# Two transformer blocks with a top-2-of-8 expert layer on one core: the first expert piece in banks 4 to 7, no scatter in the first turn, scatter halves and last transposes at other weight slots

## The chip, the core and the metric

One core of a Trainium2 chip runs the whole program. Its engines are PE (TensorE, the matrix engine), DVE (VectorE), ACT (ScalarE), POOL (GpSimd) and SP (SyncE, which here only issues DMAs). Matmul results go to PSUM, which has 8 banks of 128 x 512 float32. The metric is the device time of one execution in microseconds, lower is better.

## What is computed

Two blocks over 256 tokens of width 1024. The first has two layers of a hybrid mixer, a dense feed-forward after the first and a mixture of experts after the second. The second block has two dense feed-forwards around a mixer. The change touches the mixture of experts alone:

```python
def moe_swiglu(x, w_router, w1, w3, w2):
    logits = einsum('nd,de->ne', xf, w_router)
    top_logits, top_idx = lax.top_k(logits, 2)     # 2 of 8 experts for each token
    gates = softmax(top_logits)
    ...
    h = silu(xb @ w1[e]) * (xb @ w3[e])            # 1024 -> 3584
    y = h @ w2[e]                                  # 3584 -> 1024
    out = out.at[tok].add(y * gate)
```

## The kernel before

**Expert turns.** Each expert takes one pass over up to 128 gathered tokens, called a turn (`it` in the code, 0 to 7 here; the last has `is_last`). The weights of an expert come as 42 weight slots of 1 MB, each as two DMAs of 512 KB issued by SP into a ring of 6 buffers (`ring_data`). A slot's buffer is loaded again when PE has used it (`ring.used`). The hidden width of 3584 is cut into four pieces `c` (widths 1024, 1024, 1024, 512). An `up` slot `(c, m)` multiplies the gathered tokens by 128 rows (256 for piece 3) of w1 and w3; a `down` slot adds two 128-row parts of w2 to the expert's output. The order of a turn is written out in `Wide.TURN`: up 1 (8 slots), down 0 (4), up 2 (8), down 1 (4), up 3 (4), down 2 (4), `next` 0 (8 slots: up piece 0 of the next expert), down 3 (2). In the text "up 1,3" is slot `("up", 1, 3)`. Since a turn computes piece 0 of the next expert, piece 0 of the first expert (8 slots) stands before turn 0.

**Arithmetic of a slot.** Weights and activations are split into a high and a low part. ACT makes the high part (`weights_hi`, `e_high`, L2129), DVE the low part (`weights_lo`, `e_low`, L2456), both three slots ahead of PE (`Wide.LEAD`). PE then issues 12 matmuls of 128 x 512: 8 with the high weights (L1490 and L1491 for up, L1517 and L1518 for down), 4 with the low weights (L1494 and L1522). The 4 low ones of a slot stand in the timeline as one row "x4", so the distance from one x4 row to the next is the time of a slot.

**Banks.** An up slot accumulates in banks 0 to 3, a down slot in banks 4 and 5. Banks 6 and 7 serve all else: the gather, the transposes of a finished piece (`turn_h`, L1478), and the scatter (`scatter`, L1468 and L1469), which adds the previous expert's gated output (`Y_hi`, `Y_lo`) to the tokens by a matmul with the 0/1 matrix `chosen`. After an up piece, ACT takes the Silu of banks 0 and 1, DVE multiplies by banks 2 and 3 (`multiply`, L2915, semaphore `moe_h`), PE transposes the product, ACT and DVE copy it as high and low part (`turned`, `turned_low`, L2921, semaphore `moe_hT`).

**Where the scatter stands.** PE scatters token half 0 before slot up 1,4 and half 1 before up 1,6; both write banks 6 and 7, so the second waits until DVE has added the first to `yacc` (`add`, L2909, semaphore `y_added`). In turn 0 there is no previous expert: DVE sets `chosen`, `Y_hi` and `Y_lo` to zero before the first slots (L2977 to L2979), and turn 0 scatters zeros.

**Engines' programs.** Each engine runs its own program in order: PE, ACT and DVE each loop over turns 0 to 6 with `Fori(0, last)` and have the last turn written out behind it. `last` is read from memory into a register of each engine (`value_load`).

## Time and profile before

| | |
|---|---|
| median of 3 runs | 2168.39 us (2162.72 to 2168.89) |
| the profiled execution | 2169.8 us, of which the span from first to last instruction is 2168.0 us |
| mean granted TensorE clock | 0.990 of full |
| expert turns | from about 584 to 1562 us of the span |
| DMA in the expert turns | about 370 GB/s |

The times come from three executions; the trace is of one more. A row of the timeline is: start in us, duration in us, engine, line, operation, output<-inputs, count, and in square brackets the idle time of the engine just before, with what released it. The time shown for a matmul is longer than the distance to the next one (0.39 us against 0.227), since matmuls overlap; the distances between starts count.

### The profile page before, as it was taken

The page shows a single profiled execution, that of the slowest core. Times are in us where ns is not written, and L with a number is a line of the kernel's source. Part 1 is how long each engine was busy: PE and PEld are TensorE (multiplying, and loading weights), DVE is VectorE, ACT ScalarE, POOL GpSimd, SP SyncE. Part 2 cuts the span into 40 slices and gives each one's busy share as a digit, 9 for nine tenths or more (in the row PEclk, how much of TensorE's full clock was granted, in tenths as well). Part 3 has the DMA queues.
Part 4 walks back from the last instruction along what each step waited for, and adds up shares of the span by engine and source line. Part 5 has one row for each costly group of instructions (what it writes and reads, how often), then busy time and mean ns, then how long its engine had stood idle before and what let it go on. Part 6 is the DMA issues. An engine that isn't in the chain of part 4 may idle for free.

```text
span 2168.0 us, 31519 instructions
## 1 busy us (share of the span) xinstructions
PE 2124.3 (98%) x11901; PEld 1775.6 (82%) x11901; DVE 1594.7 (74%) x1660; ACT 1217.6 (56%) x1210; POOL 171.0 (8%) x240
## 2 busy tenths in 40 slices
PE   9999999999899999999999999999999999989998
PEld 8987888898778888888888888788778887877887
DVE  3777454567788989989898988989865439866454
ACT  4154343415467777777777777677664423664443
POOL 1200000310200000000000000000067010000000
PEclk9999999999899999999999999999999999999999
DMA  9134555412599999999999999999946564434552
GB/s 363 61 98 165 194 188 176 142 63 96 161 334 372 356 371 374 359 379 358 374 363 372 360 376 371 349 377 364 339 140 195 194 176 159 161 107 159 191 192 80
DMA packets 244403, 542.22 MB, mean 250 GB/s; under 512 B 20214, under 2 KB 122656, under 8 KB 243936
## 3 DMA queue, kind: packets, MB, share of 16 engines
q1 hardware_dynamic: 238896, 521.37, 67.3%
q0 software_dynamic: 4448, 13.79, 2.4%
q10 hardware_dynamic: 976, 5.91, 0.7%
q8 instruction: 57, 0.93, 0.2%
q14 instruction: 26, 0.21, 0.0%
HBM read 538.64 MB, written 2.36 MB: 250 GB/s over the span
## 4 chain that ended last, share of the span: by engine, by line
PE 83%; DVE 10%; issue 3%; ACT 2%; DMA 2%; SPq 0%; DVEq 0%; ACTq 0%
PE bank L1339 9%; PE bank L1341 9%; PE bank L1340 9%; PE bank L1494 8%; PE bank L1490 8%; PE bank L1491 8%; PE bank L1065 6%; PE bank L1517 4%; PE bank L1518 4%; PE bank L1522 4%; DVE weights_lo L2456 2%; PE bank L1063 2%; PE bank L1652 2%; DMA ring_data<-in_moe_w 1%; PE bank L1132 1%
## 5 line engine op out<-in xcount | busy, mean ns | idle before, releaser
L2456 DVE TENSOR_TENSOR weights_lo<-ring_data,weights_hi 128x2048 fp32r<-128x2048 f32 x336 | 760.6, 2289 | 86.4 <-ACT weights_hi L2129 85.2
L2129 ACT ACTIVATE weights_hi<-ring_data 128x2048 fp32r<-128x2048 f32 x336 | 639.8, 1920 | 183.6 <-DMA ring_data<-in_moe_w 182.5
L1490 PE MATMUL bank<-weights_hi,xg_hi 128*128 128x512 f32 x896 | 352.5, 393 | 2.6 <-DVE arena L2915 2.6
L1491 PE MATMUL bank<-weights_hi,xg_lo 128*128 128x512 f32 x896 | 349.9, 390 | 0.0
L2451 DVE TENSOR_TENSOR weights_lo<-ring_data,weights_hi 128x2048 fp32r<-128x2048 f32 x98 | 226.5, 2342 | 49.5 <-ACT weights_hi L1904 49.5
L1494 PE MATMUL bank<-weights_lo,xg_hi 128*128 128x512 f32 x896 | 240.1, 390 | 0.6 <-DVE weights_lo L2456 0.6
L1340 PE MATMUL bank<-weights_lo,xT_hi 128*128 128x512 f32 x584 | 229.5, 393 | 0.0
L1339 PE MATMUL bank<-weights_hi,xT_hi 128*128 128x512 f32 x520 | 206.2, 397 | 1.7 <-DVE bank L2504 0.9
L1341 PE MATMUL bank<-weights_hi,xT_lo 128*128 128x512 f32 x520 | 203.1, 391 | 0.0
L1490 PEld LDWEIGHTS bank<-weights_hi,xg_hi 128*128 128x128 f32 x896 | 168.7, 188 | 37.1 <-issue 3.0
L1494 PEld LDWEIGHTS bank<-weights_lo,xg_hi 128*128 128x128 f32 x896 | 168.4, 188 | 36.3 <-DVE weights_lo L2456 1.0
L1491 PEld LDWEIGHTS bank<-weights_hi,xg_lo 128*128 128x128 f32 x896 | 168.7, 188 | 34.2
L1904 ACT ACTIVATE weights_hi<-ring_data 128x2048 fp32r<-128x2048 f32 x98 | 184.0, 1918 | 0.0
L1517 PE MATMUL bank<-weights_hi,hT_hi 128*128 128x512 f32 x444 | 174.3, 393 | 0.7 <-DVE hT_lo L2921 0.7
L1518 PE MATMUL bank<-weights_hi,hT_lo 128*128 128x512 f32 x444 | 172.9, 389 | 0.0
L1871 ACT ACTIVATE arena<-bank 128x384 f32<-128x384 f32 (+5 forms) x130 | 62.8, 502 | 169.2 <-PE bank L1065 57.3
L2472 DVE TENSOR_TENSOR hT_lo<-bank,hT_hi 128x256 fp32r<-128x256 f32 x66 | 25.0, 420 | 160.0 <-ACT hT_hi L1915 159.9
L1915 ACT ACTIVATE hT_hi<-bank 128x256 fp32r<-128x256 f32 x66 | 21.8, 382 | 209.2 <-PE bank L1360 209.2
L1065 PE MATMUL bank<-actT,ring_data 128*128 128x256 f32 x608 | 136.8, 384 | 0.0
L1065 PEld LDWEIGHTS bank<-actT,ring_data 128*128 128x128 f32 x608 | 115.7, 192 | 17.0 <-issue 0.4
L1340 PEld LDWEIGHTS bank<-weights_lo,xT_hi 128*128 128x128 f32 x584 | 111.2, 190 | 22.2
L1522 PE MATMUL bank<-weights_lo,hT_hi 128*128 128x512 f32 x444 | 118.8, 389 | 0.0
(527 smaller groups left out, 3194.2 us busy)
## 6 DMA issues: line engine op xcount, KB each, us to landing
ring_data<-in_moe_w SPq DMA_DIRECT2D x672, 512.0 KB, 4.5
ring_data<-in_ffn_w_in SPq DMA_DIRECT2D x88, 512.0 KB, 4.6
ring_data<-in_w_in SPq DMA_DIRECT2D x71, 512.0 KB, 4.4
ring_data<-in_ffn_w SPq DMA_DIRECT2D x66, 512.0 KB, 4.0
ring_data<-in_ffn_w_out SPq DMA_DIRECT2D x44, 512.0 KB, 3.9
ring_data<-in_w_out SPq DMA_DIRECT2D x24, 512.0 KB, 4.6
ring_data<-in_w_in SPq DMA_DIRECT2D x8, 396.0 KB, 4.3
ring_data<-in_w_in SPq DMA_DIRECT2D x8, 390.0 KB, 5.5
```

The lines of the kernel that those rows point to most:

```text
L1065: i = mm(bk(b, 2, T)[:, g], wt[:, k, P * g:P * g + P], actT[:, k, :], start=k == 0, stop=k == DT - 1)
L1339: mm(o, x_hi, w_hi, start=start, stop=False, **kw)
L1340: mm(o, x_hi, w_lo, start=False, stop=False, **kw)
L1341: return mm(o, x_lo, w_hi, start=False, stop=stop, **kw)
L1490: mm(o, xg_hi[:, k, :], e_hi(at)[:, r], start=k == 0, stop=False)
L1491: mm(o, xg_lo[:, k, :], e_hi(at)[:, r], start=False, stop=False)
L1494: i = mm(bank[2 * part + q][:, :], xg_hi[:, k, :], e_lo(at)[:, r], start=False, stop=k == DT - 1)
L1517: mm(o, ehT_hi[:, 2 * m + f, :], w_hi[:, f, cd], start=first and f == 0, stop=False)
L1518: mm(o, ehT_lo[:, 2 * m + f, :], w_hi[:, f, cd], start=False, stop=False)
L2129: nc.scalar.activation(e_hi(at), ring_data[:, e_slot(at), :], ACT.Copy).then_inc(ring.hi_done, 1)
L2451: v.tensor_tensor(f.lo_slot(f.n0 + at), w, f.hi_slot(f.n0 + at), ALU.subtract).then_inc(f.ring.lo_done, 1)
L2456: v.tensor_tensor(e_lo(at), ring_data[:, e_slot(at), :], e_hi(at), ALU.subtract).then_inc(ring.lo_done, 1)
```

## The change

1. The first gather writes banks 0 and 1, and piece 0 of the first expert accumulates in banks 4 to 7 (`up_slot(..., 4)`). Its Silu and product read those banks.
2. Turn 0 is written out on PE and DVE (`turn(0, False, True)`), and the loops of both run from 1. PE reads `last` behind turn 0. ACT's loop still runs from 0.
3. In turn 0 the wait for the first product stands before up 1,1 and no longer before up 1,0; there are no scatters, no adds, and no memsets of `chosen`, `Y_hi`, `Y_lo`. The semaphores get their counts from other instructions.
4. On ACT and DVE the first Silu and product come behind the tenth weight split (m = 9) and no longer before it.
5. In turns 1 to 7 scatter half 0 stands before up 1,3 instead of up 1,4, and DVE's add of it moves likewise; half 1 stays before up 1,6.
6. In the last turn the transposes of piece 3 and what follows them move from slot down 2,3 to down 2,2; on ACT and DVE they come ahead of the last weight split.

```diff
-                def up_slot(c, m, at, split):
+                def up_slot(c, m, at, split, b0=0):
...
-                        o = bank[2 * part + q][:, :]
+                        o = bank[b0 + 2 * part + q][:, :]
...
-                        if part in (("up", 1, 0), ("up", 2, 0), ("up", 3, 0), ("next", 0, 0)):
+                        if part in (("up", 1, int(is_first)), ("up", 2, 0), ("up", 3, 0), ("next", 0, 0)):
...
-                        if part == ("up", 1, 4):
-                            pe.wait_ge(sem("ysb_ready"), it * 2 + 2)
-                            pe.wait_ge(sem("pgT_ready"), it + 1)
+                        if part == ("up", 1, 3) and not is_first:
+                            pe.wait_ge(sem("ysb_ready"), it * 2)
+                            pe.wait_ge(sem("pgT_ready"), it)
                             pe.wait_ge(sem("moe_hT"), it * 4 + 1)
                             scatter(0)
-                        if part == ("up", 1, 6):
+                        if part == ("up", 1, 6) and not is_first:
                             pe.wait_ge(sem("y_added"), it * 4 + 2)
                             scatter(1)
+                        if part == ("down", 0, 0) and is_first:
+                            pe.wait_ge(sem("moe_hT"), 1)
...
-                        if part == ("next", 0, 1) or (is_last and part == ("down", 2, 3)):
+                        if part == ("next", 0, 1) or (is_last and part == ("down", 2, 2)):
...
-                    up_slot(0, m, m, FFN_LOADS + m + 1)
+                    up_slot(0, m, m, FFN_LOADS + m + 1, 4)
+                turn(0, False, True)
                 pe.wait_ge(sem("dve_stage"), stage("npass_ready"))
                 last = pe.value_load(npass_i[0:1, 1:2], min_val=E - 1, max_val=2 * E - 1)
-                with pe.Fori(0, last) as it:
+                with pe.Fori(1, last) as it:
...
-                    if m == e_first + 1:
-                        silu(0, n_moe + e_first)
+                    if m == e_first + 2:
+                        silu(0, n_moe + e_first, 4)
...
+                        if is_last and (kind, c, m) == ("down", 2, 2):
+                            turned_low(3, it * 4 + 4)
...
-                        if part == ("up", 1, 4):
+                        if part == ("up", 1, 3) and not is_first:
                             add(it, 0)
...
-                v.memset(chosen.bitcast(F32)[:, :, :], 0.0).then_inc(sem("pgT_ready"), 1)
-                v.memset(Y_hi.bitcast(F32)[:, :], 0.0).then_inc(sem("ysb_ready"), 1)
-                v.memset(Y_lo.bitcast(F32)[:, :], 0.0).then_inc(sem("ysb_ready"), 1)
+                v.tensor_scalar(yacc[:, :, :], x[:, :, :], ALPHA, None, ALU.mult).then_inc(sem("y_added"), 4)
```

Three places show how instructions move. **PE, where the first piece ends and turn 0 begins.** Before, the register load and the loop's entry stand between the last matmul of the piece and up 1,0, which waits for `moe_h`:

```order
L1494 MATMUL bank3<-weights_lo_55,xg_hi_58 128x512
L1582 TENSOR_LOAD npass_i [waits dve_stage]
L1582 ISA x2
L1583 UNCONDITIONAL_BRANCH
L1583 ISA
L1483 ISA [waits moe_h]
L1490 MATMUL bank0<-weights_hi1_49,xg_hi_58 128x512 [waits weights_hi]
```

Now the piece ends in banks 4 to 7 and up 1,0 follows at once in bank 0:

```order
L1496 MATMUL bank4<-weights_lo_55,xg_hi_58 128x512 [waits weights_lo]
L1496 MATMUL bank5<-weights_lo_55,xg_hi_58 128x512
L1496 MATMUL bank6<-weights_lo_55,xg_hi_58 128x512
L1496 MATMUL bank7<-weights_lo_55,xg_hi_58 128x512
L1492 MATMUL bank0<-weights_hi1_49,xg_hi_58 128x512 [waits weights_hi]
L1493 MATMUL bank0<-weights_hi1_49,xg_lo_59 128x512
```

The wait stands one slot later, before the transposes that stand ahead of up 1,1:

```order
L1496 MATMUL bank3<-weights_lo_55,xg_hi_58 128x512
L1478 MATMUL bank6<-consts_sb,arena 128x128 [waits moe_h]
L1478 MATMUL bank6<-consts_sb,arena 128x128 x3
L1478 MATMUL bank7<-consts_sb,arena 128x128 x4
L1492 MATMUL bank0<-weights_hi1_49,xg_hi_58 128x512 [waits weights_hi]
```

The register load and the loop's entry have moved behind the last down slot of turn 0:

```order
L1524 MATMUL bank5<-weights_lo_55,hT_hi1_50 128x512
L1588 TENSOR_LOAD npass_i [waits dve_stage]
L1588 ISA x2
L1589 UNCONDITIONAL_BRANCH
L1589 ISA
L1485 ISA [waits moe_h]
L1492 MATMUL bank0<-weights_hi1_49,xg_hi_58 128x512 [waits weights_hi]
```

**DVE, the loop body, from the choice of the next tokens (L2891, now L2899) on.** Before, four low weight parts and then the add of scatter half 0 (banks 6 and 7 into `arena`):

```order
L2891 TENSOR_SCALAR arena<-consts_sb,small 128x128
L2455 REGISTER_ALU
L2456 TENSOR_TENSOR weights_lo_55<-ring_data,weights_hi1_49 128x2048 [waits weights_hi]
L2455 REGISTER_ALU
L2456 TENSOR_TENSOR weights_lo_55<-ring_data,weights_hi1_49 128x2048 [waits weights_hi]
L2455 REGISTER_ALU
L2456 TENSOR_TENSOR weights_lo_55<-ring_data,weights_hi1_49 128x2048 [waits weights_hi]
L2455 REGISTER_ALU
L2456 TENSOR_TENSOR weights_lo_55<-ring_data,weights_hi1_49 128x2048 [waits weights_hi]
L2909 TENSOR_TENSOR arena<-arena,bank6 128x512 [waits scatter_psum]
L2907 REGISTER_ALU
L2909 TENSOR_TENSOR arena<-arena,bank7 128x512 [waits scatter_psum]
```

Now three low weight parts stand ahead of the add, and the fourth follows it:

```order
L2899 TENSOR_SCALAR arena<-consts_sb,small 128x128
L2463 REGISTER_ALU
L2464 TENSOR_TENSOR weights_lo_55<-ring_data,weights_hi1_49 128x2048 [waits weights_hi]
L2463 REGISTER_ALU
L2464 TENSOR_TENSOR weights_lo_55<-ring_data,weights_hi1_49 128x2048 [waits weights_hi]
L2463 REGISTER_ALU
L2464 TENSOR_TENSOR weights_lo_55<-ring_data,weights_hi1_49 128x2048 [waits weights_hi]
L2917 TENSOR_TENSOR arena<-arena,bank6 128x512 [waits scatter_psum]
L2915 REGISTER_ALU
L2917 TENSOR_TENSOR arena<-arena,bank7 128x512 [waits scatter_psum]
L2463 REGISTER_ALU
L2464 TENSOR_TENSOR weights_lo_55<-ring_data,weights_hi1_49 128x2048 [waits weights_hi]
```

**DVE, end of the last turn.** Before, the low part of the transposed last piece (`hT_lo`) stands behind the last three low weight parts that follow the product (bank2):

```order
L2915 TENSOR_TENSOR arena<-arena,bank2 128x512 [waits moe_silu]
L2455 REGISTER_ALU
L2456 TENSOR_TENSOR weights_lo_55<-ring_data,weights_hi1_49 128x2048 [waits weights_hi]
L2455 REGISTER_ALU
L2456 TENSOR_TENSOR weights_lo_55<-ring_data,weights_hi1_49 128x2048 [waits weights_hi]
L2455 REGISTER_ALU
L2456 TENSOR_TENSOR weights_lo_55<-ring_data,weights_hi1_49 128x2048 [waits weights_hi]
L2921 TENSOR_TENSOR hT_lo1_51<-bank6,hT_hi1_50 128x512 [waits moe_hT_hi]
L2451 TENSOR_TENSOR weights_lo_55<-ring_data,first_hi_92 128x2048 [waits weights2_hi]
```

Now it stands behind two of them, and the last one follows it:

```order
L2923 TENSOR_TENSOR arena<-arena,bank2 128x512 [waits moe_silu]
L2463 REGISTER_ALU
L2464 TENSOR_TENSOR weights_lo_55<-ring_data,weights_hi1_49 128x2048 [waits weights_hi]
L2463 REGISTER_ALU
L2464 TENSOR_TENSOR weights_lo_55<-ring_data,weights_hi1_49 128x2048 [waits weights_hi]
L2929 TENSOR_TENSOR hT_lo1_51<-bank6,hT_hi1_50 128x512 [waits moe_hT_hi]
L2463 REGISTER_ALU
L2464 TENSOR_TENSOR weights_lo_55<-ring_data,weights_hi1_49 128x2048 [waits weights_hi]
L2459 TENSOR_TENSOR weights_lo_55<-ring_data,first_hi_92 128x2048 [waits weights2_hi]
```

## Rows read from the trace of the kernel before

**Rows 1.** The page, the chain of work that ended last, by engine:

```profile
PE 83%; DVE 10%; issue 3%; ACT 2%; DMA 2%; SPq 0%; DVEq 0%; ACTq 0%
```

**Rows 2.** Windows; last three columns: granted clock, DMA share, GB/s:

```profile
610.00:620.00 10.00, 10.00 (x43) 8.17 (x43) 9.78 (x12) 8.05 (x6) 0.00 (x0) 0.84 0.58 185
640.00:740.00 100.00, 100.00 (x464) 83.19 (x463) 88.32 (x55) 75.06 (x54) 1.07 (x1) 1.00 1.00 375
870.00:880.00 10.00, 9.86 (x44) 7.82 (x43) 8.90 (x8) 5.92 (x5) 0.00 (x0) 1.00 0.84 304
```

**Rows 3.** Timeline of PE where the loop goes from turn 0 to 1:

```profile
731.05 1.07 PE L1522 MATMUL bank<-weights_lo,hT_hi 128*128 128x512 f32 x4
733.77 1.07 PE L1494 MATMUL bank<-weights_lo,xg_hi 128*128 128x512 f32 x4
```

**Rows 4.** Timeline of DVE ahead of its first weight parts:

```profile
587.41 0.27 DVE L2977 MEMSET chosen<- 128x256 f32 x1
...
589.74 15.44 DVE L2456 TENSOR_TENSOR weights_lo<-ring_data,weights_hi 128x2048 fp32r<-128x2048 f32 x7
```

**Rows 5.** Timeline of PE, first piece and start of turn 0:

```profile
588.59 1.07 PE L1494 MATMUL bank<-weights_lo,xg_hi 128*128 128x512 f32 x4
592.02 1.19 PE L1494 MATMUL bank<-weights_lo,xg_hi 128*128 128x512 f32 x4 [0.56 <-DVE weights_lo L2456]
...
605.77 1.07 PE L1494 MATMUL bank<-weights_lo,xg_hi 128*128 128x512 f32 x4
609.41 0.52 PE L1490 MATMUL bank<-weights_hi,xg_hi 128*128 128x512 f32 x1 [2.57 <-DVE arena L2915]
...
616.56 1.07 PE L1494 MATMUL bank<-weights_lo,xg_hi 128*128 128x512 f32 x4
```

**Rows 6.** Timeline of ACT around the first Silu (L2146):

```profile
601.42 1.28 ACT L2146 ACT_TABLE_LOAD   x1
606.88 1.08 ACT L2146 ACTIVATE arena<-bank 128x512 f32<-128x512 f32 x2 [4.18 <-PE bank L1494]
```

**Rows 7.** Timeline of PE around scatters, turns 0, 1, 2 and 6:

```profile
622.00 1.07 PE L1494 MATMUL bank<-weights_lo,xg_hi 128*128 128x512 f32 x4
...
625.63 1.07 PE L1494 MATMUL bank<-weights_lo,xg_hi 128*128 128x512 f32 x4
...
749.20 1.07 PE L1494 MATMUL bank<-weights_lo,xg_hi 128*128 128x512 f32 x4
751.31 0.50 PE L1468 MATMUL bank<-Y_hi,chosen 128*128 128x512 f32 x1 [1.04 <-DVE arena L2909]
...
754.21 1.07 PE L1494 MATMUL bank<-weights_lo,xg_hi 128*128 128x512 f32 x4
...
871.39 1.07 PE L1494 MATMUL bank<-weights_lo,xg_hi 128*128 128x512 f32 x4
...
875.45 1.07 PE L1494 MATMUL bank<-weights_lo,xg_hi 128*128 128x512 f32 x4
...
1356.19 1.07 PE L1494 MATMUL bank<-weights_lo,xg_hi 128*128 128x512 f32 x4
...
1361.84 1.07 PE L1494 MATMUL bank<-weights_lo,xg_hi 128*128 128x512 f32 x4
```

**Rows 8.** Timeline of DVE, turn 1 (add of half 0) and turn 6:

```profile
749.98 1.28 DVE L2909 TENSOR_TENSOR arena<-arena,bank 128x512 f32<-128x512 f32 x2
...
1346.17 1.28 DVE L2921 TENSOR_TENSOR hT_lo<-bank,hT_hi 128x512 fp32r<-128x512 f32 x2
```

**Rows 9.** Timeline of PE, end of the last turn:

```profile
1553.21 1.08 PE L1522 MATMUL bank<-weights_lo,hT_hi 128*128 128x512 f32 x4
1555.03 0.49 PE L1517 MATMUL bank<-weights_hi,hT_hi 128*128 128x512 f32 x1 [0.74 <-DVE hT_lo L2921]
...
1556.97 1.07 PE L1522 MATMUL bank<-weights_lo,hT_hi 128*128 128x512 f32 x4
```

**Rows 10.** Timeline of DVE, first instruction behind DVE's own register load:

```profile
580.36 0.18 DVE L2877 TENSOR_TENSOR small<-small 128x16 f32<-128x16 f32 x1 [1.53 <-issue]
```

More of the change, by code:

```diff
@@ L925, in _ @@
             pool.wait_ge(sem("gather_psum"), 2)
-            pool.wait_ge(sem("pgT_ready"), 2)
+            pool.wait_ge(sem("pgT_ready"), 1)
             with pool.Fori(0, last) as it:
@@ L929, in _ @@
                 pool.wait_ge(sem("gather_psum"), it * 2 + 4)
-                pool.wait_ge(sem("pgT_ready"), it + 3)
+                pool.wait_ge(sem("pgT_ready"), it + 2)
             layer_norm_params(3)
@@ L1447, in gather_first @@
                             for j in range(TT):
-                                i = mm(bk(6 + b, 4, CAP)[:, d], x[:, j, P * (4 * b + d):P * (4 * b + d + 1)], Pm[:, j, :], start=j == 0, stop=j == TT - 1)
+                                i = mm(bk(b, 4, CAP)[:, d], x[:, j, P * (4 * b + d):P * (4 * b + d + 1)], Pm[:, j, :], start=j == 0, stop=j == TT - 1)
                         i.then_inc(sem("gather_psum"), 1)
@@ L1473, in scatter, with turn_h @@
                         scatter_half(j, q, 6)
-                def turn_h(c):
+                def turn_h(c, is_first=False):
                     for q in range(Wide.WIDTHS[c] // P):
                         i = nc.tensor.transpose(bk(6 + q // 4, 4, P)[:, q % 4], eh[:, P * q:P * q + P], ident)
+                        if is_first and q == 0:
+                            i.then_inc(sem("scatter_psum"), 4)
                     i.then_inc(sem("moe_hT_psum"), 1)
-                def up_slot(c, m, at, split):
+                def up_slot(c, m, at, split, b0=0):
                     pe.wait_ge(ring.hi_done, split)
@@ L1493, in up_slot @@
                     for k, part, q, r in work:
-                        i = mm(bank[2 * part + q][:, :], xg_hi[:, k, :], e_lo(at)[:, r], start=False, stop=k == DT - 1)
+                        i = mm(bank[b0 + 2 * part + q][:, :], xg_hi[:, k, :], e_lo(at)[:, r], start=False, stop=k == DT - 1)
                     i.then_inc(ring.used, 1)
@@ L1523, in down_slot, with turn @@
                     i.then_inc(ring.used, 1)
-                def turn(it, is_last):
+                def turn(it, is_last, is_first=False):
                     for s, (kind, c, m) in enumerate(Wide.slots(is_last)):
@@ L1586, in moe @@
                 for q in range(2):
-                    pe.wait_ge(sem("ysb_ready"), last * 2 + 3 + q)
+                    pe.wait_ge(sem("ysb_ready"), last * 2 + 1 + q)
                     for j in range(TT):
@@ L2136, in moe, with gathered, silu @@
                 last = act.value_load(npass_i[0:1, 1:2], min_val=E - 1, max_val=2 * E - 1)
-                def gathered(it):
+                def gathered(it, b0=6):
                     for b in range(2):
                         act.wait_ge(sem("gather_psum"), it * 2 + b + 1)
-                        a_(xg_hi[:, 4 * b:4 * b + 4, :], bk(6 + b, 4, CAP), ACT.Copy, "xg_hi")
-                def silu(c, used):
+                        a_(xg_hi[:, 4 * b:4 * b + 4, :], bk(b0 + b, 4, CAP), ACT.Copy, "xg_hi")
+                def silu(c, used, b0=0):
                     act.wait_ge(ring.used, used)
                     for q in range(Wide.WIDTHS[c] // 512):
-                        i = nc.scalar.activation(esil[:, 512 * q:512 * q + 512], bank[q][:, :], ACT.Silu)
+                        i = nc.scalar.activation(esil[:, 512 * q:512 * q + 512], bank[b0 + q][:, :], ACT.Silu)
                     i.then_inc(sem("moe_silu"), 1)
@@ L2175, in turn @@
                                 gathered(it + 1)
-                        if part == ("next", 0, 0) or (is_last and part == ("down", 2, 3)):
+                        if part == ("next", 0, 0):
                             turned(3, it * 4 + 4)
@@ L2922, in turned_low, with turn @@
                     i.then_inc(sem("moe_hT"), 1)
-                def turn(it, is_last):
+                def turn(it, is_last, is_first=False):
                     slots = Wide.slots(is_last)
@@ L2927, in turn @@
                     for s, (kind, c, m) in enumerate(slots):
+                        if is_last and (kind, c, m) == ("down", 2, 2):
+                            turned_low(3, it * 4 + 4)
                         if not is_last or s + Wide.LEAD < n:
@@ L2937, in turn @@
                                 choose(it + 1)
-                        if part == ("up", 1, 4):
+                        if part == ("up", 1, 3) and not is_first:
                             add(it, 0)
-                        if part == ("up", 1, 6):
+                        if part == ("up", 1, 6) and not is_first:
                             add(it, 1)
@@ L2949, in turn @@
                                 gathered(it + 1)
-                        if part == ("next", 0, 0) or (is_last and part == ("down", 2, 3)):
+                        if part == ("next", 0, 0):
                             turned_low(3, it * 4 + 4)
@@ L2974, in moe @@
                 dve.wait_ge(sem("dve_stage"), stage("norm_rows2"))
-                st.do(v.tensor_scalar(yacc[:, :, :], x[:, :, :], ALPHA, None, ALU.mult))
-                v.memset(chosen.bitcast(F32)[:, :, :], 0.0).then_inc(sem("pgT_ready"), 1)
-                v.memset(Y_hi.bitcast(F32)[:, :], 0.0).then_inc(sem("ysb_ready"), 1)
-                v.memset(Y_lo.bitcast(F32)[:, :], 0.0).then_inc(sem("ysb_ready"), 1)
+                v.tensor_scalar(yacc[:, :, :], x[:, :, :], ALPHA, None, ALU.mult).then_inc(sem("y_added"), 4)
+                dve.wait_ge(sem("y_added"), 4)
                 st.settle()
                 for m in range(2, e_first + Wide.LEAD):
-                    if m == e_first + 1:
-                        multiply(0, 1)
+                    if m == e_first + 2:
+                        multiply(0, 1, 6)
                     e_low(m, FFN_LOADS + m + 1)
-                with dve.Fori(0, last) as it:
+                turn(0, False, True)
+                with dve.Fori(1, last) as it:
                     turn(it, False)
```

20 lines of the change are left out of this document (11 added, 9 removed).

## Prediction

> **What bounds the kernel now.** I read the page's chain of waits first: PE holds 83% of it [rows 1], so the question is where PE's own stream has holes. Then the windows: in the expert turns the DMA engines are also busy to 1.00 at 375 GB/s over a long stretch [rows 2], so a second bound stands close behind. The timeline of PE decides between them. Its weight slots follow one another at 2.72 us (731.05 to 733.77, [rows 3]), whether the slot is an up or a down one, and a slot with transposes or a scatter half ahead of it takes 3.63 (622.00 to 625.63, [rows 7]), 0.91 more. Whatever is above these two numbers is a stall, and there are few. After a stall the DMA share falls (0.84 at 870 to 880, 0.58 at 610 to 620, [rows 2]), since all ring buffers are full and wait for PE: there PE is late, not the data. So a hole closed in PE's stream shortens the run, as far as the DMA engines can follow.
>
> **The change part by part.** I sum the holes.
>
> *The memsets.* DVE's first low weight part starts at 589.74, behind memsets that began at 587.41 [rows 4]. PE waits for it: 588.59 to 592.02 is 3.43 us instead of 2.72 [rows 5]. Without the memsets DVE starts up to 2.3 us earlier, more than the 0.71 that is missing. Gain 0.7 (bounds 0.5, if the new wait on `y_added` delays DVE a little, and 0.71).
>
> *The first product.* Before, PE ends the first piece, stands idle 2.57 us for Silu and product, and starts up 1,0 at 609.41. It then runs cold: the granted clock of 610 to 620 is 0.84 as a mean [rows 2], which is a part of that stretch at 1.2 GHz, after an idle PE. From the piece's last x4 row at 605.77 to that of up 1,1 at 616.56 are 10.79 us [rows 5]; one plain slot and one with transposes would be 2.72 + 3.63 = 6.35. The hole is 4.44. In the changed kernel PE has up 1,0 to do while ACT and DVE work, 2.72 us against 2.57 of waiting, so the transposes before up 1,1 find the product just ready, if ACT and DVE are free. ACT must now also make high part m = 9 before the Silu. It stood idle 4.18 us after the table load of 1.28 [rows 6], and a high part takes about 1.9: it fits if the data have landed. I take the whole 4.4; bounds 3.4 (product 1 us late, no cold stretch) and 4.4.
>
> *No scatter in turn 0.* Two halves of 0.91 each: 1.8. Nothing else needs them. DVE also loses four adds, which is cover and no gain.
>
> *Scatter half 0 one slot earlier.* The wait of half 1 for DVE's add of half 0 costs in turn 1: 749.20 to 754.21 is 5.01, 1.38 above 3.63. In turn 2, 871.39 to 875.45 is 4.06, 0.43 above; turns 3, 4 and 5 show the same pattern with about 0.36 each. In turn 6, 1356.19 to 1361.84 is 5.65, 2.02 above [rows 7]; turn 7 has none. Together 4.9. DVE did the add behind four low weight parts, now behind three, and one takes 15.44 / 7 = 2.2 us [rows 4]: the add comes 2.2 earlier, and the largest hole is 2.02. In turn 1 the add would end at 749.98 + 1.28 - 2.2 = 749.1 [rows 8], PE comes at 749.20 + 0.91 = 750.1. What is late next: half 0 itself now starts one slot earlier and needs `hT_lo` out of banks 6 and 7. Tightest in turn 6: `hT_lo` ends at 1346.17 + 1.28 = 1347.45 [rows 8], and PE would come at 1357.10 less three slots and a scatter, 9.07, thus at 1348.03 [rows 7], 0.6 to spare. The low part that the add now precedes comes 1.28 later, two slots before its use. Gain 4.9, bounds 3 and 4.9.
>
> *Last transposes one slot earlier.* In the last turn PE waits 0.74 for `hT_lo`, and 1553.21 to 1556.97 is 3.76, 1.04 above 2.72 [rows 9]. DVE now makes it before its last weight part of 2.2 us, more than the hole. Gain 1.0; bounds 0.5 and 1.04, since the data of the last slots land just in time.
>
> Holes together: 0.7 + 4.4 + 1.8 + 4.9 + 1.0 = 12.8.
>
> *What is taken off.* First, the data. The hole at the first product left the DMA engines idle: 185 GB/s of 375 in 610 to 620 is 5.1 us unused [rows 2]. PE gains 4.4 and 1.8 there, 6.2 in all, so relative to PE the data fall about 1.1 behind. From up 1,1 of turn 0 (616.56, [rows 5]) to up 1,0 of turn 1 (733.77, [rows 3]) PE took 117.2 us; with one slot with transposes more, 3.63, a turn is 120.8, and without the scatters 119.0. The 42 MB slots and the rows for the next expert, 44.6 MB, take 44.6 / 0.375 = 118.9 us. Nearly equal, so the lag of 1.1 stays until turn 1. The parts are made three slots ahead and most of that is hidden: I take off 0.5, bounds 0 and 2. In turns 1 to 6 PE needs 120.8 a turn against the same 118.9, which leaves room for the holes to close.
>
> Second, PE's register load and the loop's entry. They stood inside the 2.57 us of idle time, now they stand between turn 0 and turn 1 in a full stream. No row shows such a load on PE in the open. The nearest is DVE's, with 1.53 us before its next instruction [rows 10], part of it a wait of DVE on its own result. The other bound is 0: PE's sequencer runs ahead of the array, and the loop's back edge costs nothing, 2.72 us over it [rows 3]. I take 0.3, nearer the row on PE itself.
>
> The Trainium skill, "TensorE: Matmul & The Clock Gate", its opening table, gives TensorE a queue 64 entries deep. By that a load of about 1 us would be hidden whenever the weights are ready that far ahead; the trace shows only the free back edge.
>
> Sum: 12.8 - 0.5 - 0.3 = 12.0. The profiled execution took 2169.8, of which 1.8 lies around the span; with the change 2157.8. The median of the runs is 1.4 lower, 2168.4, so I predict 2156.4.
>
> **The rivals.** *The data become the bound (chance 0.17).* If the DMA engines reach only 370 GB/s in turn 0, the turn takes 120.5 instead of 119.0, and the lag of 1.1 comes on top. PE then waits for low weight parts, up to 3 us, and the late DVE start of turn 1 leaves part of its 1.4 us scatter wait. Gain 12.0 - 4 = 8: 2160.4. For it speaks a share of 1.00; against it that PE shows no wait for weights after 592.
>
> *The product is late (0.08).* If the data for m = 9 land after about 605, the split delays the Silu by up to a slot, and PE idles and runs cold as before, one slot later. The 4.4 are lost: gain 7.6, 2160.8. Against it: 4.18 us of ACT's idle time.
>
> *The earlier half 0 waits (0.10).* If `hT_lo` comes later than 0.6 to 2 us against PE, the scatter hole moves from half 1 to half 0 and most of the 4.9 is not gained: gain 7 to 8, and with the data lag only 5 to 6: 2162 to 2163.
>
> *The loop costs (0.04).* The Trainium skill, "Runtime: NRT & Kernel Launch", section "Instruction fetch mechanics", says that a taken branch out of the fetched window stalls for a fetch. As a mechanism here: entry into the loop behind a much longer straight program, on PE and DVE. Its price would be the 1.53 of [rows 10] once, or at each of the six passes 9 us: gain 3, 2165. The free back edge [rows 3] speaks against it, for the body has hardly changed its length.
>
> *Slower (0.03).* Half 0's new wait grows past the point where PE's clock falls. The hole at the first product shows the price, 2.57 idle and 4.44 in all; in seven turns that is 31 us, less the 12 gained: 2187. It decides only if `hT_lo` comes about 3 to 4.5 us later than now in each turn; DVE's order before it has not changed.
>
> The rest, 0.58, is the forecast.
>
> **How the numbers follow.** 0.3%, 6.5 us, is about what a measurement of this kernel can tell from no change. The forecast and the first two rivals lie beyond it (0.58 + 0.17 + 0.08), of the third not quite half: 0.84 less a little for the unforeseen, 0.82 faster; 0.14 the same; 0.04 slower. The three runs before spread over 6.2 us, more than any bound here, so the range takes in more than the sum: below, all 12.8 and half of that spread, 2151; above, the third rival with some noise, 2165.
>
> **What would show it.** In the changed kernel's timeline of PE: no hole at 592; the first piece's last x4 row, the next after 2.72 us and the next after 3.63, at full clock; no L1468 in turn 0; the slot with half 1 at 3.63 in turns 1 to 6; 2.72 over the loop's entry (a hole there prices the load); 2.72 for down 3,0 in the last turn. The DMA share of the first 100 us of turn 0 should be 1.00 without the gap. Waits of L1496 for `weights_lo` would show the data rival. I am wrong if PE waits anew for weights or for `hT_lo` in most turns.

## The result and the profile after

The changed kernel takes 2154.19 us (median of 6 runs, 2151.72 to 2158.26) against 2166.01 us (6 runs, 2162.72 to 2168.89): ratio 0.9947, 95% interval 0.9937 to 0.9957, thus 11.8 us by the medians and 9.3 to 13.6 by the interval. The forecast was 2156.4 us, 12.0 below the 2168.39 of the three runs known then; the six runs of the kernel before stand 2.4 lower, so the gains are what to compare. The profiled execution took 2158.26 us, 11.5 less than that of before.

The page of the changed kernel, chain of work that ended last, and from the costliest groups the x4 matmuls on low weight parts of up slots (busy, mean ns | idle before):

```profile
PE 92%; DVE 6%; ACT 1%; issue 1%; DMA 0%; DVEq 0%; SPq 0%; ACTq 0%
...
L1496 PE MATMUL bank<-weights_lo,xg_hi 128*128 128x512 f32 x896 | 239.8, 389 | 0.0
```

PE's share rose from 83% [rows 1] to 92%, and PE never waits for a low weight part in any up slot. The windows, as in [rows 2]:

```profile
610.00:620.00 10.00, 10.00 (x49) 8.21 (x49) 9.38 (x13) 9.07 (x8) 0.00 (x0) 1.00 0.99 366
640.00:740.00 100.00, 100.00 (x464) 83.22 (x463) 89.60 (x60) 75.44 (x54) 2.13 (x1) 1.00 1.00 374
870.00:880.00 10.00, 10.00 (x45) 8.28 (x45) 9.72 (x9) 7.09 (x6) 0.00 (x0) 1.00 0.95 344
```

In 610 to 620 the clock is 1.00 instead of 0.84, and the DMA share 0.99 instead of 0.58. The timeline of PE, first piece and turn 0:

```profile
587.60 1.07 PE L1496 MATMUL bank<-weights_lo,xg_hi 128*128 128x512 f32 x4
590.32 1.07 PE L1496 MATMUL bank<-weights_lo,xg_hi 128*128 128x512 f32 x4
593.04 1.07 PE L1496 MATMUL bank<-weights_lo,xg_hi 128*128 128x512 f32 x4
...
606.64 1.07 PE L1496 MATMUL bank<-weights_lo,xg_hi 128*128 128x512 f32 x4
609.36 1.07 PE L1496 MATMUL bank<-weights_lo,xg_hi 128*128 128x512 f32 x4
610.30 1.06 PE L1478 MATMUL bank<-consts_sb,arena 128*128 128x128 f32 x8
613.05 1.08 PE L1496 MATMUL bank<-weights_lo,xg_hi 128*128 128x512 f32 x4
```

Where [rows 5] have 3.43, 3.64 of idle and first matmul, and a slow slot, there are 2.72, 2.72, 2.72 and 3.69. Over the loop's entry and through turn 1:

```profile
725.69 1.07 PE L1524 MATMUL bank<-weights_lo,hT_hi 128*128 128x512 f32 x4
728.41 1.07 PE L1496 MATMUL bank<-weights_lo,xg_hi 128*128 128x512 f32 x4
...
734.75 1.07 PE L1496 MATMUL bank<-weights_lo,xg_hi 128*128 128x512 f32 x4
735.65 0.39 PE L1468 MATMUL bank<-Y_hi,chosen 128*128 128x512 f32 x1
...
743.81 1.07 PE L1496 MATMUL bank<-weights_lo,xg_hi 128*128 128x512 f32 x4
744.72 0.39 PE L1468 MATMUL bank<-Y_hi,chosen 128*128 128x512 f32 x1
...
747.44 1.07 PE L1496 MATMUL bank<-weights_lo,xg_hi 128*128 128x512 f32 x4
```

The register load stands in the 2.72 from 725.69 to 728.41, and cannot be seen. The slot with half 1 takes 747.44 - 743.81 = 3.63, against 5.01 in [rows 7]. DVE in the same place:

```profile
732.21 1.28 DVE L2929 TENSOR_TENSOR hT_lo<-bank,hT_hi 128x512 fp32r<-128x512 f32 x2
...
741.45 1.27 DVE L2917 TENSOR_TENSOR arena<-arena,bank 128x512 f32<-128x512 f32 x2
```

`hT_lo` ends at 733.49, 2.16 ahead of half 0 (735.65), and the add at 742.72, 2.00 ahead of half 1 (744.72). The two margins are 2.14 to 2.16 and 1.99 to 2.00 in all of turns 1 to 6; in turn 7 the second is 2.61, since DVE has no next tokens to choose there. In the last turn slot down 3,0 takes 2.72 instead of 3.76 [rows 9]:

```profile
1542.83 1.07 PE L1524 MATMUL bank<-weights_lo,hT_hi 128*128 128x512 f32 x4
1545.55 0.62 PE L1524 MATMUL bank<-weights_lo,hT_hi 128*128 128x512 f32 x2
```

**The measure used below.** Let the stage length be the time from the x4 row of the first weight slot to that of slot down 3,0 of the last turn, 334 slots later. Before it is 1556.97 - 585.87 = 971.10, after 1545.55 - 587.60 = 957.95: 13.15 less. The rest of the execution varies more than the terms asked about: 1191.6 to 1198.4 us of span outside the stage over all 14 profiles (2156.3 - 957.95 = 1198.35 for the changed kernel, the longest). So single terms are read from the stage, hole by hole; whole times only back up the larger ones. A hole is what a slot takes above its usual time (2.72, or 3.62 with a scatter half or the first transposes ahead of it); it holds the listed idle time of PE and what is lost behind it. PE is called cold where its granted clock stands at the lower of its two levels, 1.2 GHz, and warm at the upper one. One of e1's eleven executions took 2378.78 us at a granted clock of 0.846, a slow one, and is left out of its ratio and of the median given here.

### The profile page after: what moved, and what is told of

Read it like the earlier page. It is cut to its first block, busy times and chain, and to the rows that moved or that the text cites. A ratio compares the mean times of both kernels' runs of the same rounds, so it can differ in the third digit from the quotient of the medians.

```text
span 2156.3 us, 31393 instructions
## 1 busy us (share of the span) xinstructions
PE 2119.3 (98%) x11893; PEld 1774.7 (82%) x11893; DVE 1588.5 (74%) x1653; ACT 1217.9 (56%) x1210; POOL 170.6 (8%) x240
## 3 DMA queue, kind: packets, MB, share of 16 engines
HBM read 538.64 MB, written 2.36 MB: 251 GB/s over the span
## 4 chain that ended last, share of the span: by engine, by line
PE 92%; DVE 6%; ACT 1%; issue 1%; DMA 0%; DVEq 0%; SPq 0%; ACTq 0%
PE bank L1492 9%; PE bank L1493 9%; PE bank L1496 9%; PE bank L1339 9%; PE bank L1341 9%; PE bank L1340 9%; PE bank L1065 6%; PE bank L1520 5%; PE bank L1519 5%; PE bank L1524 5%; PE bank L1063 2%; PE bank L1658 2%; PE bank L1478 1%; PE bank L1132 1%; PE bank L1360 1%; PE bank L1151 1%
```

## The experiments

| run | stage length us | median us (runs) |
|---|---|---|
| before | 971.10 | 2166.82 (22, beside the first four) |
| changed | 957.95 | 2154.19 (6) |
| e1 half 0 alone | 966.67 | 2162.06 (10) |
| e2 first piece in banks 0 to 3 | 960.76 | 2155.85 (5) |
| e3 half 0 one slot earlier still | 965.14 | 2162.00 (11) |
| e4 half 0 back | 962.89 | 2158.47 (6) |
| e5 memsets back | 958.99 | 2154.77 (1) |
| e6 nine register loads | 961.16 | 2159.41 (1) |
| e7 banks 0 to 3 and memsets | 963.33 | 2160.12 (1) |
| e8 as e2 | 961.34 | 2157.01 (1) |
| e9 as e2, 17 loads | 972.82 | 2168.64 (1) |
| e10 memsets, scatters of turn 0, last transposes back | 962.55 | 2158.29 (1) |
| e11 as e7 | 963.30 | 2158.07 (1) |
| e12 first Silu one split earlier | 959.34 | 2154.52 (1) |

Beside the single runs the kernel before took 2164.86 us (e5 to e8) and 2165.92 us (e9 to e12), once each.

### e1: half 0 alone, on the kernel before

```diff
-                        if part == ("up", 1, 4):
+                        if part == ("up", 1, 3):
```

on PE (scatter) and DVE (add).

> The kernel before with one part of the change alone: scatter half 0 and DVE's add of it stand ahead of up 1,3 instead of up 1,4, in all eight turns. Measured is the length of the expert stage, from the x4 row of the first weight slot to that of slot down 3,0 of the last turn, 971.10 us in the kernel before. Theory (the six holes at half 1 are DVE's late add and close one for one): 4.9 shorter, 966.2, half 1's slots at 3.62 in every turn, all other holes (592, first product, last turn) as before. Rival 1 (half 0 waits in its new place, or the low part behind the add comes late): less than 3.5 shorter, with the missing time in slots up 1,3 to up 1,5. Rival 2 (the holes are the data's, since half 1's turns are long only where the weights are late too): within 1 us of 971.1, the holes seen again a slot or two on.

Measured 966.67, 4.43 less; ratio to before 0.998 (0.9971 to 0.999). All six holes at half 1 are gone (slots 3.62 to 3.63 in eight turns), worth 4.98 by the intervals, and nothing took their place in the turns. But the last turn's hole grew, from 0.74 of idle time [rows 9] to 1.36:

```profile
1549.04 0.49 PE L1517 MATMUL bank<-weights_hi,hT_hi 128*128 128x512 f32 x1 [1.36 <-DVE hT_lo L2921]
```

so its slot took 4.37 where before it took 3.76: 0.61 was given back. The theory holds for half 1 and both rivals fall, but its "all other holes as before" does not hold for the last one. ACT and DVE of this run, ahead of that row:

```profile
1544.06 1.92 ACT L2129 ACTIVATE weights_hi<-ring_data 128x2048 fp32r<-128x2048 f32 x1 [0.54 <-DMA ring_data<-in_moe_w]
```

```profile
1546.01 2.29 DVE L2456 TENSOR_TENSOR weights_lo<-ring_data,weights_hi 128x2048 fp32r<-128x2048 f32 x1 [0.15 <-ACT weights_hi L2129]
1548.22 0.68 DVE L2921 TENSOR_TENSOR hT_lo<-bank,hT_hi 128x512 fp32r<-128x512 f32 x1
```

`hT_lo` stands behind a low part that waits for ACT, which waits for its data. PE, 5 us earlier in the stage than before, had come closer to the data.

### e4: half 0 back to its old place, on the changed kernel

```diff
-                        if part == ("up", 1, 3) and not is_first:
+                        if part == ("up", 1, 4) and not is_first:
```

> The changed kernel with half 0 and its add ahead of up 1,4 again, as in the kernel before, in turns 1 to 7. Stage length in the changed kernel 957.95. Theory A (the holes of the kernel before, 1.38 in its turn 1, 2.02 in turn 6 and about 0.4 in the rest, belong to the order of DVE's work in that place): 4.9 longer, 962.9, hole by hole. Theory B (the 0.4 belongs to the order, but the 1.38 and 2.02 to one late weight part in that execution, which another execution has elsewhere or not): 2.2 to 3 longer, 960.2 to 961, with about 0.36 in each of six turns.

Measured 962.89, 4.94 more. The sum is that of A, but the pattern is that of B: the slots with half 1 are 0.41, 0.43, 0.91, 0.41, 1.13, 0.40 and 1.24 above 3.62 in turns 1 to 7, where before had 1.39, 0.44, 0.37, 0.37, 0.38, 2.03 and 0. Some 0.4 belongs to the order; 0.5 to 1.6 come on top in whichever turns DVE has been held up. (In the last turn DVE has about 0.6 us less to do ahead of the add, the choice of the next tokens, and the kernel before had no hole there.) In the largest hole of either kernel it is a late weight part. DVE's rows some 20 us ahead of it, in turn 6 of the kernel before and in turn 7 of e4:

```profile
1332.32 2.29 DVE L2456 TENSOR_TENSOR weights_lo<-ring_data,weights_hi 128x2048 fp32r<-128x2048 f32 x1 [1.98 <-ACT weights_hi L2129]
```

```profile
1446.33 2.29 DVE L2464 TENSOR_TENSOR weights_lo<-ring_data,weights_hi 128x2048 fp32r<-128x2048 f32 x1 [1.20 <-ACT weights_hi L2135]
```

ACT had waited for the weights in memory there, 2.36 and 1.57 us, and DVE does not catch up before the add: before, `hT_lo` starts 1356.19 - 1346.17 = 10.02 us ahead of the x4 row of up 1,5 in turn 6, against 871.39 - 859.83 = 11.56 in turn 2, so it is 1.54 late, and the hole is 1.59 larger. That the two sums agree (4.93 and 4.98) is luck. PE in turn 7 of e4:

```profile
1467.80 1.07 PE L1496 MATMUL bank<-weights_lo,xg_hi 128*128 128x512 f32 x4
1469.81 0.50 PE L1468 MATMUL bank<-Y_hi,chosen 128*128 128x512 f32 x1 [0.93 <-DVE arena L2917]
...
1472.66 1.07 PE L1496 MATMUL bank<-weights_lo,xg_hi 128*128 128x512 f32 x4
```

The idle time is 0.93 and the hole 1.24. A difference of this kind comes back in every warm stall: 1.36 and 1.65 in e1, 2.50 and 2.79 in e2, 0.55 and 0.80 to 0.84 in e3, and, the smallest, 0.35 and 0.56 ahead of the last transposes in e6. A warm stall of PE costs its idle time and 0.2 to 0.35 more.

### e3: half 0 one slot earlier still

```diff
-                        if part == ("up", 1, 3) and not is_first:
+                        if part == ("up", 1, 2) and not is_first:
```

> The changed kernel with half 0 and its add one slot earlier still, ahead of up 1,2, in turns 1 to 7. In the changed kernel hT_lo, which must have left banks 6 and 7, ends 2.16 us before half 0 in turn 1, and a slot is 2.72. Theory: half 0 then waits 0.6 us in each of seven turns for hT_lo, or somewhat more since DVE's add now stands ahead of a low part that PE wants sooner: stage length 957.95 + 4 = 962, between 961 and 964. Rival 1 (DVE finishes hT_lo earlier relative to PE in later turns, so only turn 1 waits): 958 to 959. Rival 2 (the idle PE falls to the low clock each time): some 2 us a turn more, 972 or above.

Measured 965.14, 7.2 more, above the range of 961 to 964. The whole-kernel time agrees (2162.0, 7.8 more). PE and DVE in turn 1 and in turn 4:

```profile
732.85 0.47 PE L1468 MATMUL bank<-Y_hi,chosen 128*128 128x512 f32 x1 [0.55 <-DVE hT_lo L2929]
...
1099.07 0.47 PE L1468 MATMUL bank<-Y_hi,chosen 128*128 128x512 f32 x1 [1.91 <-DVE hT_lo L2929]
```

```profile
731.42 1.28 DVE L2929 TENSOR_TENSOR hT_lo<-bank,hT_hi 128x512 fp32r<-128x512 f32 x2
...
1083.82 2.29 DVE L2464 TENSOR_TENSOR weights_lo<-ring_data,weights_hi 128x2048 fp32r<-128x2048 f32 x1 [0.88 <-ACT weights_hi L2135]
1086.32 2.29 DVE L2464 TENSOR_TENSOR weights_lo<-ring_data,weights_hi 128x2048 fp32r<-128x2048 f32 x1 [0.20 <-ACT weights_hi L2135]
...
1097.64 1.29 DVE L2929 TENSOR_TENSOR hT_lo<-bank,hT_hi 128x512 fp32r<-128x512 f32 x2
```

The wait is the one worked out, 2.72 - 2.16 = 0.56, measured 0.55; I had left out the 0.25 to 0.3 on top, in seven turns. Six turns lose 0.80 to 0.84, and turn 4 loses 2.21, where two late weight parts pushed DVE back by 0.88 + 0.20. The clock did not fall (rival 2). The place chosen by the change is thus the only one of three without a wait: earlier PE waits for `hT_lo`, later for the add.

### e2, e7, e8, e11: the first product

```diff
-                        if part in (("up", 1, int(is_first)), ("up", 2, 0), ("up", 3, 0), ("next", 0, 0)):
+                        if part in (("up", 1, 0), ("up", 2, 0), ("up", 3, 0), ("next", 0, 0)):
...
-                    up_slot(0, m, m, FFN_LOADS + m + 1, 4)
+                    up_slot(0, m, m, FFN_LOADS + m + 1)
```

and the gather, Silu and product in the matching banks. e8 is the same kernel; e7 and e11 are it with the three memsets back.

> The changed kernel with the first expert's first piece in banks 0 to 3 again, the gather's product in banks 6 and 7, and the wait for Silu and product ahead of up 1,0; turn 0 stays written out and without scatter. Stage length in the changed kernel 957.95 us. Theory: the hole of the kernel before comes back whole, some 2.6 us of idle PE and the rest as a low granted clock behind it, 4.4 in all: 962.4. Rival 1 (only the idle time comes back, the clock stays up because less stands between): 960.5. Rival 2 (the hole lets the ring of weights fill, and PE then never waits, while the changed kernel loses part of its gain to late data further on): 961 or less with the hole at 4.4.

> The second experiment's kernel once more, unchanged, for a second profile of the first product's hole. Theory A (it has no cold stretch because only one stall stands there): hole 2.8 again, clock 1.00, stage length 960.8. Theory B (chance of where the idle time falls): hole 2.8 or 4.4.

> The kernel of the second experiment (first piece in banks 0 to 3, wait ahead of up 1,0), which stood idle 2.50 us with a hole of 2.79 and no cold stretch, with the three memsets back, so that PE also has its stall of 0.7 us at the second weight slot some 15 us earlier, as in the kernel before. Theory A (the cold stretch of the kernel before, 1.7 us of its 4.45, needs both stalls): the hole at the first product is 4.4 again and the granted clock falls there below 0.9. Theory B (the cold stretch comes or stays away by where the idle time falls, whatever stood ahead): it is 2.8 or 4.4 with no bearing on the memsets; together with the repeated run beside it this shows how far one kernel's profile varies here. The memsets' own part is 0.9 in either case.

> The seventh experiment's kernel (first piece in banks 0 to 3, memsets back) once more, for a second profile of the first product's hole, which was 4.39 with a granted clock of 0.71 behind it. Theory A (the stall of 0.8 us at the second slot and the idle time at the product together bring the cold stretch): 4.4 again. Theory B (chance of where the idle time falls): 2.8 or 4.4.

Measured holes at the first product: e2 2.79 (stage 960.76), e8 2.78, e7 4.39, e11 4.37. In e2 the theory (4.4, 962.4) missed, and its rival 1 came (960.5: the idle time without the low clock); e8 repeats it. (e8's stage is 0.6 longer than e2's by a wait for the last turn's product, its slot with the last transposes taking 3.82 instead of 3.23; e6 and e12 have such a wait too, 0.56 and 0.27.) So far theory A looked right. But e9, which has no memsets either, gives a third profile of e2's hole, and there it is 4.40. PE in e2 and in e9:

```profile
605.83 0.50 PE L1492 MATMUL bank<-weights_hi,xg_hi 128*128 128x512 f32 x1 [2.50 <-DVE arena L2923]
```

```profile
608.20 0.50 PE L1492 MATMUL bank<-weights_hi,xg_hi 128*128 128x512 f32 x1 [2.49 <-DVE arena L2939]
```

and the windows of e2 and e9 (third column from the right is the granted clock):

```profile
605.00:615.00 10.00, 9.17 (x44) 7.70 (x45) 9.28 (x13) 8.31 (x7) 0.00 (x0) 1.00 0.75 254
```

```profile
605.00:615.00 10.00, 7.51 (x31) 5.72 (x30) 5.94 (x5) 5.97 (x7) 0.00 (x0) 0.83 0.65 232
```

The idle time is the same, 2.50 and 2.49; the clock is 1.00 in one and 0.83 in the other, and the hole 2.79 or 4.40. Theory A falls: one stall is enough. e2's rival 1 is no rule either. What remains is that the hole is 2.79 without the cold stretch and 4.4 with it. Of seven profiles with this idle time (before, e1, e2, e7, e8, e9, e11) five have the cold stretch. What decides between them stays open. With the memsets all four profiles are cold (before, e1, e7, e11), without them one of three (e9), so a bearing of the memsets on the odds isn't excluded.

### e5: memsets back

```diff
+                v.memset(chosen.bitcast(F32)[:, :, :], 0.0)
+                v.memset(Y_hi.bitcast(F32)[:, :], 0.0)
+                v.memset(Y_lo.bitcast(F32)[:, :], 0.0)
```

> The changed kernel with DVE's three memsets put back where they stood, ahead of its low weight parts; nothing else uses them. Theory (they delay the first low part that PE waits for): the x4 rows of the second and third weight slot come 3.4 and 2.9 instead of 2.72 after the one before, stage length 957.95 + 0.86 = 958.8, or up to 1.1 with what a stall costs beyond the idle time. Rival (PE's first slot in the changed kernel is later against DVE than before, so that they hide): 958.0.

Measured 958.99, 1.04 more: the second and third slot come after 3.54 and 2.87, 0.97 above 2.72. The theory holds.

### e6 and e9: the register load

```diff
+                last = pe.value_load(npass_i[0:1, 1:2], min_val=E - 1, max_val=2 * E - 1)
```

eight times more in e6, sixteen times in e9 (the latter on e2's kernel).

> The changed kernel with nine register loads on PE instead of one between turn 0 and the loop. The changed kernel shows 2.72 us over that place, as over any plain slot. Theory (PE's sequencer runs ahead of the array, and a load of about 1 us each disappears in that lead): if the lead is several us long, nine loads of at most 1.5 us are 13 us, more than a lead of two to five us, and the hole is somewhere from 5 to 10 us; the price of one load in the sequencer is then (hole + lead) / 9. Rival 1 (a register load on PE is far cheaper than DVE's 1.53 us row): hole 0 with all nine. Rival 2 (the forecast's 0.3 for each load in the open, hidden in the changed kernel by chance): 8 times 0.3 = 2.4 us, stage length 960.4.

> The second experiment's kernel (first piece in banks 0 to 3) with seventeen register loads on PE between turn 0 and the loop, at another place than the hole it has. Nine loads left PE idle 2.31 us there (hole 2.61), one load 0. Theory (each load takes a fixed time p of the sequencer, PE's lead hides the first of it): the hole grows by 8 p against nine loads; with p between 0.33 (no lead at all) and 1.5 us (DVE's row) it is 5.3 to 14.6 us, and lead = 9 p - 2.3. Rival (what costs is not the load but the code that it pushes apart, once): the hole stays near 2.6. It is also a third profile of the first product's hole without the memsets: theory A (two stalls are needed for the cold stretch) 2.8, theory B (chance) 2.8 or 4.4.

PE behind turn 0 in e6 and in e9:

```profile
727.26 0.49 PE L1492 MATMUL bank<-weights_hi,xg_hi 128*128 128x512 f32 x1 [2.31 <-issue]
```

```profile
736.63 0.79 PE L1492 MATMUL bank<-weights_hi,xg_hi 128*128 128x512 f32 x1 [7.53 <-issue]
```

Eight loads more add 7.53 - 2.31 = 5.22 us of idle time, 0.65 each. Going back along this line, 9/8 x 5.22 - 2.31 = 3.56 us of loads are hidden by PE's lead, net of whatever else the sequencer has to do there; one load fits five times. e6 by itself did not decide: its hole of 2.61 is below the theory's 5 to 10 and close to the 2.4 of rival 2 (0.3 each); only rival 1 (free loads) fell there. e9 decides: 0.3 each would add 2.4 of idle time, not 5.22, and e9's rival falls too. The theory's mechanism, a lead that hides the first loads, holds, with 0.65 us for a load and not about 1. The 0.65 assumes that e6's and e9's kernels have the same lead. The single hidden load costs 0. After the 7.53 us PE also ran cold (granted clock 0.50 in 733 to 738 and 0.57 in 738 to 743): up 1,0 came 12.18 after the slot before it and up 1,1 4.63 after that, 10.5 above the usual 2.72 and 3.62.

The Trainium skill, "DMA: Bandwidth & Descriptors", section "Latency and other measured facts", gives `tensor_load` a floor of about 600 ns. The register load is a TENSOR_LOAD in PE's program, with two more instructions of its line behind it, and the 0.65 agrees with that floor. The Trainium skill's queue of 64 entries ("TensorE: Matmul & The Clock Gate", opening table) is neither shown nor refuted by a lead of 3.56 us, since that is net of other work of the sequencer.

### e10: memsets, turn 0's scatters and the last transposes back

```diff
+                        if is_first and part in (("up", 1, 3), ("up", 1, 6)):
+                            pe.wait_ge(sem("moe_hT"), 1)
...
-                        if part == ("next", 0, 1) or (is_last and part == ("down", 2, 2)):
+                        if part == ("next", 0, 1) or (is_last and part == ("down", 2, 3)):
```

with both halves' matmuls behind that wait, the memsets, and the matching places on ACT and DVE; the four adds of turn 0 are left out.

> The changed kernel with three things put back in three separate places: the three memsets (known to cost 0.97 by the fifth experiment, and now needed), both scatter halves of turn 0 on PE, of zero data, without DVE's adds of them, and the last turn's transposes, with high and low part of hT, one slot later. Theory: the slots with halves in turn 0 take 3.62 instead of 2.72, 1.8 for both; the slot down 3,0 of the last turn takes 3.76 instead of 2.72, 1.04 more, or 1.65 as in the first experiment's profile: stage length 957.95 + 0.97 + 1.8 + 1.04 = 961.8, up to 962.4. Rival (the data set the turn's length, so that 1.8 of PE's work in turn 0 is hidden by waits that close): the slots take 3.62, but no later slot can become shorter than 2.72, so that this rival needs waits in the changed kernel that its profile does not show; 960.0.

Measured 962.55, 4.6 more: 0.99 at the memsets, 0.91 for each half (slots of 3.63), and 1.80 in the last turn, whose slot took 4.52. The rival falls, for nothing of the 1.8 came back. The last hole is larger than expected: 1.04, 1.65, 1.80 in before, e1 and e10, as the stage ahead of it had lost 0, 5.0 (half 1) and 9.4 us (half 1 and first product) of holes. DVE's `hT_lo` stands behind low parts that come with the data, and the data don't come earlier because PE does. These are three single profiles; how much this hole varies between executions of one kernel was not measured, so that it grows for this reason is argued and not shown. PE in e10:

```profile
1546.16 0.49 PE L1519 MATMUL bank<-weights_hi,hT_hi 128*128 128x512 f32 x1 [1.50 <-DVE hT_lo L2932]
```

### e12: first Silu one weight split earlier

```diff
-                    if m == e_first + 2:
+                    if m == e_first + 1:
```

on ACT and DVE.

> The changed kernel with ACT's first Silu and DVE's first product one weight split earlier, ahead of part m = 9 instead of m = 10. The changed kernel's slot with the first transposes is 3.69, 0.07 above the others of its kind. Theory (the product is ready in time, and the 0.07 is how PE takes a tile fresh from DVE): the product comes up to 2 us earlier, the slot stays within 0.1 of 3.62, and nothing else moves, 957.9 to 958.0. Rival 1 (the product was late by 0.07, so that an earlier one gives it back): 3.62. Rival 2 (high part m = 9, now behind the Silu, comes too late for PE at up 1,1): a hole of some tenths to 2 us in that slot.

Measured 959.34, 1.4 more. The slot with the transposes stayed at 3.69, but that decides nothing between theory and rival 1, for the product did not come earlier against PE: Silu waits for PE's last matmuls in both kernels and starts 1.10 us behind the piece's last x4 row (604.89 - 603.79 here, 607.75 - 606.64 in the changed kernel). In e2 and e8, whose product is ready a slot ahead of the transposes, the same slot takes 3.61 and 3.62. So the 0.07 goes with a product that is only just ready; whether it is a wait is open. And later slots came after 2.82, 3.54 and 2.89, 1.09 above 2.72 in all; the last transposes took another 0.27. ACT and PE of e12:

```profile
604.89 1.09 ACT L2152 ACTIVATE arena<-bank 128x512 f32<-128x512 f32 x2 [4.53 <-PE bank L1496]
605.86 5.53 ACT L2135 ACTIVATE weights_hi<-ring_data 128x2048 fp32r<-128x2048 f32 x3
```

```profile
619.28 1.21 PE L1496 MATMUL bank<-weights_lo,xg_hi 128*128 128x512 f32 x4 [0.66 <-DVE weights_lo L2464]
```

ACT idles 4.53 us waiting for PE, with a high part queued behind the Silu (and DVE 4.20 us, with the low part behind the product), and this backlog reaches PE as a late low part in the fifth slot. That is rival 2, three slots later than I had placed it. In the changed kernel the same part goes first, and ACT idles 2.12:

```profile
602.40 1.92 ACT L2135 ACTIVATE weights_hi<-ring_data 128x2048 fp32r<-128x2048 f32 x1 [0.54 <-DMA ring_data<-in_moe_w]
...
607.75 1.09 ACT L2152 ACTIVATE arena<-bank 128x512 f32<-128x512 f32 x2 [2.12 <-PE bank L1496]
```

Fed by this order, PE has no hole at all. The edit that the prediction treated as a condition ("it fits if the data have landed") is itself worth about 1.1, by this one profile.

## Why the prediction was right, and where it was off

*The sum of the holes, 12.8.* Right, and a little low: by the intervals of the profile before, 0.71 + 0.15 (memsets) + 4.45 (first product) + 1.82 (scatters) + 4.98 (half 1) + 1.04 (last transposes) = 13.15, and 13.15 is what the stage lost. Every hole named closed, and only the 0.07 at the first transposes is new.

*The memsets, 0.7.* The term left out the 0.15 of the third slot; together 0.86 in [rows 5]'s profile, 0.97 when they are put back (e5).

*The first product, 4.4.* Closed whole in the profiles compared. 2.8 came in every profile with this idle time, and 1.6 more with the cold stretch, in five of seven. So the mean over executions may be smaller than 4.4; by how much isn't shown, since all four profiles with the memsets in place were cold. The mechanism was right: PE has up 1,0 to do in the meantime. The size belongs to one kind of execution.

*No scatter in turn 0, 1.8.* 0.91 for each half, on its own (e10).

*Half 0 one slot earlier, 4.9.* The stage lost 4.4 on the kernel before (e1) and gains 4.9 back on the changed one (e4). The margins were larger than worked out: 2.00 for the add against 1.0, and 2.16 for `hT_lo` against the 0.6 of turn 6, since both had been worked out from turns in which a late weight part held DVE up. The large holes of turns 1 and 6 were no property of those turns, as e4 shows.

*Last transposes, 1.0.* Right in the pair of profiles, but 1.65 and 1.80 where other holes are closed and this is not. Terms were added as if independent; this one was larger where the others had gone. The new place has a wait of its own in some executions, for the last turn's product: 0.62, 0.56 and 0.27 in e8, e6 and e12, at most 0.07 in the other profiles.

*Taken off for the data, 0.5.* Wrong: 0. From up 1,1 of turn 0 to up 1,0 of turn 1 PE took 728.41 - 613.05 = 115.36, just 117.2 - 1.8, at a DMA share of 1.00. If the data fell 1.1 behind, the parts made ahead hid it; no run shows the lag itself.

*Taken off for the register load and loop entry, 0.3.* Wrong for the whole: 0. The load costs 0.65 in the open (e6, e9), below the 1.53 of [rows 10] and inside PE's lead. The loop is entered at 2.72, with no stall. The Trainium skill ("Runtime: NRT & Kernel Launch", "Instruction fetch mechanics") charges a taken branch out of the fetched window with a fetch; this stream shows no such cost, and no run shows whether the branch left the window.

*The rivals.* The data did not become the bound: PE shows no wait for weights in turn 0 or later. The product was not late beyond 0.07. The loop cost nothing. The earlier half 0 does not wait where it stands, but one slot earlier it does (e3). The slow rival fell: half 0 had no wait, and even in e3 PE's clock stayed up over idle times of 0.55 to 1.91 us. Two small sums of the prediction are off, without weight for the forecast: its chances for faster add up to about 0.87 by its own words, not 0.84, and all 12.8 with half of the spread give 2152.5 as the lower end, not 2151.

*The total.* 13.15 in the stage and 11.8 by the medians are both within 9.3 to 13.6; the forecast's 12.0 met the medians more closely than its terms deserve. It took off 0.8 that nothing cost, and allowed nothing for executions in which the first product's hole is smaller, nor for the waits of the last product. What makes the medians' gain 1.4 smaller than the stage's in one pair of profiles isn't shown; that the 0.8 went in the same direction is luck.

## What to carry to other kernels

Measure holes as the distance between like instructions, not by the idle time: here each stall of PE cost 0.2 to 0.35 us more than the idle time listed, and one of 2.5 us up to 1.6 more by the clock. When a late hole hangs on data, expect it to grow as the holes ahead of it close (1.04, 1.65 and 1.80 in three profiles), and do not add up edits of one stage as if they were independent. Behind an in-order engine's long wait stands everything else queued on it: put the work that another engine needs next ahead of such a wait (e12, 1.1 us), and a scatter where all that it waits for is ready: here one place of three, with some 2 us to spare on both sides.

## What was not expected of the hardware

- The same idle time of 2.5 us on PE led to a granted clock of 0.83 in a 10 us window in one profile and of 1.00 in another; the hole was 4.40 or 2.79. Over seven profiles with this idle time it was low in five. Why is open.
- A register load on PE takes 0.65 us of its sequencer (from idle times of 2.31 with nine loads and 7.53 with seventeen), and by the same line some 3.6 us of such work disappear behind a full stream of matmuls.
- An idle PE loses 0.25 to 0.35 us more than its idle time at full clock, after 0.55 as after 2.50 us, ahead of a 128x512 matmul; ahead of the last transposes (128x128) it was 0.21, after 0.35 and 0.41 us.
